# QKV projection of a two-layer trunk: from one product of full matrices to seven products of halves

## What is computed

```python
for i in range(DEPTH):
    hn = rmsnorm(h, attn_norm[i])
    qkv = hn @ w_qkv[i]                                   # 2304 columns
    aq, ak, av, bq, bk, bv, _rest = jnp.split(qkv, QKV_SPLITS + (QKV_WIDTH,), axis=-1)
    ya = sliding_window_sink_attention(aq, ak, av, ...)   # QK-norm, partial rotary (group A)
    yb = chunked_relpos_attention(bq, bk, bv, ...)        # QK-norm, bias by relative position (group B)
    h = h + jnp.concatenate([ya, yb], axis=-1) @ w_o[i]
    h = h + conv_gated_mlp(rmsnorm(h, ffn_norm[i]), w_up[i], conv_w[i], conv_b[i], w_down[i])
    gate = jax.nn.sigmoid(rmsnorm(h, ple_norm[i]) @ w_ple_gate[i])
    h = h + (p[i] @ w_ple_proj[i]) * gate
```

## Time and profile before

| | |
|---|---|
| median of 3 runs | 2497.51 us (2496.66 to 2498.68) |
| the profiled execution | 2496.49 us, its span 2494.7 us |
| PE busy | 2460.4 us, 99% of the span |
| PEld / DVE / ACT / POOL busy | 86% / 54% / 51% / 41% |
| TensorE clock granted | 0.999 of full, 9 in all 40 slices |
| QKV stage, layer 0 | first product at 14.53, last of the four entry transpositions at 220.03 |
| QKV stage, layer 1 | first product about 1253.4, last entry transposition at 1459.60 |

### The profile page before, as it was taken

How to read it: one execution, slowest core, us unless ns; L and a number is a source line. 1 busy time by engine, 2 the same in 40 slices (tenths; PEclk the granted TensorE clock), 3 DMA queues, 4 the chain that set the end, 5 groups by cost and what they waited for, 6 DMA issues and landing times.

```text
span 2494.7 us, 37383 instructions
## 1 busy us (share of the span) xinstructions
PE 2460.4 (99%) x12992; PEld 2150.7 (86%) x12992; DVE 1348.7 (54%) x1876; ACT 1263.3 (51%) x1966; POOL 1034.8 (41%) x783
## 2 busy tenths in 40 slices
PE   8999999999999999999999999999999999999999
PEld 8999998878888888888899999988788888888887
DVE  3114664376656668873341146733856656778732
ACT  4335773465555554344353467734655555533342
POOL 3455241158788850001224442412578878400011
PEclk9999999999999999999999999999999999999999
DMA  4112000313333358431111120003133243573312
GB/s 166 45 51 55 20 15 26 118 51 109 111 95 109 94 172 294 124 109 43 45 39 45 50 53 28 10 26 127 48 112 109 80 125 110 183 268 123 99 46 84
DMA packets 187901, 225.61 MB, mean 90 GB/s; under 512 B 16112, under 2 KB 118896, under 8 KB 187792
## 3 DMA queue, kind: packets, MB, share of 16 engines
q1 hardware_dynamic: 187200, 221.69, 28.1%
q0 software_dynamic: 592, 2.46, 0.3%
HBM read 169.08 MB, written 55.36 MB: 90 GB/s over the span
## 4 chain that ended last, share of the span: by engine, by line
PE 86%; DVE 5%; ACT 4%; issue 3%; POOL 1%; DMA 0%; ACTq 0%; DVEq 0%; POOLq 0%; SPq 0%
PE ps L2179 10%; PE ps L2181 10%; PE ps L2180 10%; PE ps L2637 10%; PE ps L2639 10%; PE ps L2640 10%; PE ps L2663 6%; PE ps L2661 6%; PE ps L2662 6%; PE ps L2413 3%; PE ps L2402 1%; PE ps L2374 1%; PE ps L2506 1%; PE ps L2331 1%; PE ps L2473 1%
## 5 line engine op out<-in xcount | busy, mean ns | idle before, releaser
L885 POOL TENSOR_TENSOR w_hl<-w_raw,w_hl 128x1024 fp32r<-128x1024 f32 x84 | 203.1, 2418 | 989.5 <-ACT w_hl L1076 989.5
L2179 PE MATMUL ps<-w_hl,xT 128*128 128x384 f32 (+1 forms) x1280 | 460.1, 359 | 3.1 <-POOL w_hl L885 1.0
L2181 PE MATMUL ps<-w_hl,xT 128*128 128x384 f32 (+1 forms) x1280 | 456.3, 356 | 0.0
L2180 PE MATMUL ps<-w_hl,xT 128*128 128x384 f32 (+1 forms) x1280 | 456.0, 356 | 0.0
L1076 ACT ACTIVATE w_hl<-w_raw 128x1024 fp32r<-128x1024 f32 x84 | 89.1, 1060 | 430.5 <-PE ps L2181 404.7
L2179 PEld LDWEIGHTS ps<-w_hl,xT 128*128 128x128 f32 x1280 | 240.3, 188 | 24.4 <-issue 2.5
L2181 PEld LDWEIGHTS ps<-w_hl,xT 128*128 128x128 f32 x1280 | 240.2, 188 | 20.2
L2180 PEld LDWEIGHTS ps<-w_hl,xT 128*128 128x128 f32 x1280 | 240.4, 188 | 19.1
L2009 DVE SCALAR_TENSOR_TENSOR ps<-c_up,ccols,ps 128x1023 f32<-128x1023 f32 x84 | 107.8, 1283 | 142.3 <-ACT ps L1430 142.3
L1666 DVE TENSOR_REDUCE q_sum<-sq 128x384 f32 x80 | 44.2, 553 | 251.4 <-ACT sq L1138 251.4
L1988 DVE TENSOR_TENSOR c_up<-ps,kept 128x512 f32<-128x512 f32 x126 | 86.6, 689 | 125.1 <-ACT kept L1389 69.4
(11 more groups left out here) (292 smaller groups left out, 6087.1 us busy)
## 6 DMA issues: line engine op xcount, KB each, us to landing
ad_raw<-v_rows SPq DMA_DIRECT2D x70, 512.0 KB, 3.7
raw_a<-in_w_up SPq DMA_DIRECT2D x44, 512.0 KB, 5.0
raw_g<-in_w_up SPq DMA_DIRECT2D x44, 512.0 KB, 5.3
v_rows<-c_up SPq DMA_DIRECT2D x22, 1024.0 KB, 4.4
w_raw<-in_w_qkv SPq DMA_DIRECT2D x48, 384.0 KB, 3.2
wd_main<-in_w_down SPq DMA_DIRECT2D x30, 512.0 KB, 8.1
v_rows<-hc_g SPq DMA_DIRECT2D x22, 512.0 KB, 5.0
w_raw<-in_w_o SPq DMA_DIRECT2D x16, 512.0 KB, 3.8
```

The lines of the kernel that those rows point to most:

```text
L885: nc.gpsimd.tensor_tensor(w_hl[:, slot % 2, 1, :], w_raw[:, slot % 2, :], w_hl[:, slot % 2, 0, :].bitcast(F), ALU.subtract) \
L2179: nc.tensor.matmul(dst, lhs[:, k, 0, cols], wh, start=first, stop=False)
L2180: nc.tensor.matmul(dst, lhs[:, k, 0, cols], wl, start=False, stop=False)
L2181: return nc.tensor.matmul(dst, lhs[:, k, 1, cols], wh, start=False, stop=last)
```

## The change

The matrix of inputs is cut in quarters A11 (first 512 tokens, first 512 features) to A22, the weights in quarters B11 (first 512 rows, first 1152 columns) to B22, the result in C11 to C22, and C is made from seven products (Strassen's) in the order of `Q_ORDER`. Each product has three steps of 384 columns (21 steps, `m`), each step two slots (42 slots), and each slot 24 matmuls: 4 tiles of tokens, 6 matmuls each. A step fills 4 banks, the next step the other 4.

- Weights: 30 of the 42 slots need the sum or difference of two blocks. SP loads both (384 KB each), POOL sums them in place (`qkv_sum`), then ACT makes the high part and POOL the low part. The first block has three buffers (`w_raw` and the new `w_raw_c`), the second two. The order on POOL is: low of slot s, then sum of slot s+2. Ops of a slot are now 128x768, no longer 128x1024.
- Inputs: h transposed and scaled is kept whole in `x_keep`; for the products 5, 7, 1, 2 and 6 POOL forms the sum of two quarters in two parts (`input_sum`, 128x1024 each), ACT makes the high part (`input_high`) and DVE the low (`input_low`), into a ring of three. Product 4 needs a plain quarter (no sum), product 3 uses A11.
- Results: of each step ACT writes what comes first into a block of C (`first_writes`), DVE adds the rest (`q_add`, 128x384, from PSUM onto the block). Squares are now taken from the finished block in SBUF (`head_squares`).
- The norm's factors of the QK-norm are made in two parts, heads 0 to 23 and the rest.
- `rotate` moves from the projection into group B, two tiles behind the copies of each of the heads 1 to 4. POOL's low of the first slot of `w_o` now stands between the copies of head 0 and those of head 1. The loads of group A's values (`load_values`) move behind the bias of the last head; the load of `ext_in` moves from POOL's queue to SP's.

```diff
-SLOTS = QCHUNKS * 4 + 8 + 10
+Q_ORDER = (3, 5, 7, 4, 1, 2, 6)
+Q_WEIGHTS = {3: ("B12", "B22"), 5: ("B22",), 7: ("B21", "B22"), 4: ("B21", "B11"), 1: ("B11", "B22"),
+             2: ("B11",), 6: ("B11", "B12")}
+Q_INPUTS = {5: ("A11", "A12", 1), 7: ("A12", "A22", -1), 1: ("A11", "A22", 1), 2: ("A21", "A22", 1),
+            6: ("A21", "A11", -1)}
+Q_FIRST = {3: (("C12", 1), ("C22", 1)), 5: (("C11", -1),), 4: (("C21", 1),)}
+Q_ADDS = {5: (("C12", 1),), 7: (("C11", 1),), 4: (("C11", 1),), 1: (("C11", 1), ("C22", 1)),
+          2: (("C21", 1), ("C22", -1)), 6: (("C22", 1),)}
+Q_FINAL = {5: "C12", 1: "C11", 2: "C21", 6: "C22"}
+QSTEPS = 7 * Q_CHUNKS
+O0 = 2 * QSTEPS
...
+            def load_qkv(L, slot):
+                names, n = Q_WEIGHTS[q_product(slot // 2)], q_twos(slot)
+                if len(names) == 2:
+                    if L * Q_TWO + n >= 2:
+                        sp.wait_ge(s_w_sum, L * Q_TWO + n - 1)
+                    sp.dma_start(other_raw(slot).rearrange("p (k n) -> p k n", k=2), qkv_block(L, slot, names[1])) \
+                        .then_inc(other_loaded[slot % 2], 16)
+                sp.wait_ge(s_w_low_ready, L * SLOTS + (slot + 1 if slot < 2 else slot))
+                sp.dma_start(one_raw(slot).rearrange("p (k n) -> p k n", k=2), qkv_block(L, slot, names[0])) \
+                    .then_inc(one_loaded[slot % 3], 16)
...
+                qkv_sum(0)
+                qkv_sum(1)
+                for slot in range(O0):
+                    qkv_low(slot)
                     if slot in between:
                         between[slot]()
+                    if slot % 6 == 2 and slot < O0 - 6 and Q_ORDER[slot // 6 + 1] in Q_INPUTS:
+                        input_sum(2 * (slot // 6 + 1))
+                    if slot and slot % 6 == 0 and Q_ORDER[slot // 6] in Q_INPUTS:
+                        input_sum(2 * (slot // 6) + 1)
+                    if slot + 2 < O0:
+                        qkv_sum(slot + 2)
...
+                def copies(hd):
+                    b = hd % 2
+                    pool.wait_ge(s_fill_ready, L * FILLS + (4 * hd + C_FILL - 4))
+                    if hd == 1:
+                        pool.wait_ge(s_q_rstd_ready, L * 2 + 2)
...
+                for hd in range(B_HEADS):
+                    copies(hd)
+                    if hd == 0:
+                        low(O0)
+                    if 1 <= hd <= TT // 2:
+                        rotate(2 * hd - 2)
+                        rotate(2 * hd - 1)
...
+                for m in range(1, QSTEPS - 1):
+                    qkv_high(L, 2 * m + 1)
+                    first_writes(m - 1)
+                    head_squares(m - 1)
...
+                    qkv_high(L, 2 * m + 2)
+                    if m % 3 and m < QSTEPS - 3:
+                        input_high(2 * (m // 3 + 1) + m % 3 - 1)
...
+                for m in range(1, QSTEPS):
+                    step_adds(m - 1)
+                    i = 2 * (m // 3 + 1)
+                    if m % 3 == 0 and m > 1:
+                        input_low(2 * (m // 3) + 1)
+                    if m < QSTEPS - 1:
+                        step_rest(m - 1)
+                    if m % 3 == 1 and i < 14:
+                        input_low(i)
...
+                for m in range(1, QSTEPS):
+                    for kp in range(2):
+                        slot_ready(2 * m + kp)
+                        if m % Q_CHUNKS == 0:
+                            pe.wait_ge(s_xlow, L * XFILLS + input_number(2 * (m // Q_CHUNKS) + kp))
                         for t in range(4):
+                            if kp == 0:
+                                q_bank_free(m, t)
+                            q_row(m, kp, t)
```

More of the change, by code:

```diff
@@ new lines, in step_rest, with q_mean, q_refined @@
+                def step_rest(m):
+                    for t in range(4):
+                        if len(Q_ADDS.get(q_product(m), ())) > 1:
+                            q_add(m, 1, t)
+                        if q_normed(m):
+                            head_sum(m, t)
+                def q_mean(part, heads):
+                    nc.vector.tensor_scalar(q_sum[:, :, heads], q_sum[:, :, heads], 1.0 / HD, EPS, ALU.mult, ALU.add) \
+                        .then_inc(s_q_mean_ready, 1)
+                def q_refined(part, heads):
+                    dve.wait_ge(s_q_rms_ready, L * 2 + part + 1)
+                    refine(q_rstd[:, :, heads], q_sum[:, :, heads], q_tmp[:, :, heads], 1 + part).then_inc(s_q_rstd_ready, 1)
```

582 lines of the change are left out of this document (392 added, 190 removed).

## The result

Changed kernel: median 2527.36 us (2525.12 to 2530.93, 4 runs); before, on the same chip, 2497.40 (2496.66 to 2498.68, 4 runs). Ratio 1.0121, 95% interval 1.0108 to 1.0134: slower by 30 us, where 7 were forecast, and above the range. The profiled execution took 2526.32 us.

A forecast was written before the change was run, and what follows sets the result against it. PE, busy 99% of the span, was taken as the bound. Layer 0 +2.3 - 1.5 + 4.4 = +5.2, layer 1 +0.8 - 2.2 + 4.4 = +3.0, less 1.0: +7, so 2503.7 profiled, 2504.5 median, range 2490 to 2515.

The forecast's parts named there:

- The waits: Projection, mostly product starts and slot 3: PE waits 12.4 + 5.3 + 4.7 = 22.4 us per layer.
- 204.0: Projection stage length after the change: 174.7 + 5.1 + 1.8 + 22.4 = 204.0 us.
- 48 matmuls take 8.32 us, one 0.1733: Projection: each matmul less saves 0.173 us while helpers keep pace; 25.0 us per layer if PE never waits.
- half a microsecond was to be caught up: Group B: PE has little slack, so half a microsecond of loss per layer is recovered, 1.0 in all.
- Step 1: Slots 3 and 4 wait for the norm's factor: 3.9 us at slot 3 and 0.8 at slot 4.
- Sharing: Product starts: DVE's input low parts and POOL's operations exclude each other on SBUF, 5.3 us more per layer.
- The exit: Projection's end: last entry transposition to first for head 1 takes 8.4 us instead of 4.0, losing 4.4 per layer.
- Rotations at nothing: Group B: rotations, 7.0 us per head, fit in POOL's idle 11.2 before the values' copy, costing nothing.
- late loads: Rival, projection: weight loads land after 4.5 us; at 5.3 the kernel takes 2515 us; chance 0.13.
- POOL did not keep up: Rival, product starts: POOL's operations cost less than scaled, so the waits vanish; 2469 us, chance 0.1.
- the end was not caught up: Rival, projection's end: the wait there is caught up in head 0; -7.8, 2497 us, chance 0.15.
- the sharing was there: Rival, projection: the sharing wait is absent or falls where POOL waits anyway; -10.6, 2494 us, chance 0.17.

The follow-up runs named there:

- experiment 1: Changed kernel with idle TensorE matmuls or transpositions put into its long gaps, no wait removed: 2512.5 us, ratio 1.0060.
- experiment 5: Changed kernel with DVE's low parts of the input sums reading one SBUF operand instead of two: 2519.5 us, ratio 1.0088.

## Why the prediction was wrong

**The waits: right in place and kind, near in size.** Products 7 and 1 wait for DVE, 4.25 and 3.64, the others 1.1 to 1.6, all in the places named. With the clock kept up (experiment 1) the stages are 204.8 and 202.2 against 204.0, but in layer 0 two misses cancel: from slot 2 on a layer has 20.7 us over 4.16 a slot where 22.4 were forecast, and the first two slots of layer 0 have 8.1 (5.4 in layer 1), 2.7 more than in layer 1, which no term of the sum held.

**The step that failed: what a wait costs.** "48 matmuls take 8.32 us, one 0.1733" was read from a kernel in which PE never stood still for long, and the stage was summed as matmuls at that price plus waits. A wait of 3.6 to 5.2 us costs 1.7 to 2.7 more (16.6 over seven of them), as the matmuls in the part of the stretch behind it run at 0.32. Against the 204.0 forecast the stages are 8.3 and 7.3 longer. The first head of each layer is 1.6 longer (17.3 for 15.7) with its 3.4 us at half clock, where half a microsecond was to be caught up and none was. No rival had this mechanism.

The rest of the 22.6 us between 2503.7 and the profiled 2526.3 is small: the exits 0.8 and 0.9, the first product 0.3, the 1.0 that was to be caught up, 0.3 at the end, and 0.6 at the start of layer 1. That last one hides a misreading: before, layer 1's first product starts at 1254.12, not 1253.4, and the stage is 205.5 long, not 206.2:

```profile
1254.12 0.41 PE L2179 MATMUL ps<-w_hl,xT 128*128 128x384 f32 x1 [0.71 <-issue]
```

Counted from head 2 of layer 0, the product now comes 0.7 later, where the forecast in effect had 0.1 (1253.4 + 0.8).

**Step 1: mis-sized.** 3.9 and 0.8 were forecast, 5.2 and about 0 came. Of the 1.6 that the factor came late, 0.8 is the last copy and square (the mean starts 1.7 behind the step's start, for 0.9) and 0.75 the chain from mean to factor, 4.95 for 4.2. The 4.2 was no undisturbed figure either. It has this row, which the earlier trace rows leave out, beside POOL's low part that runs from 36.46 to 38.85:

```profile
36.75 2.13 DVE L1612 TENSOR_TENSOR h_tmp<-h_rms 128x8 f32<-128x8 f32 x1
```

Before, one of the small operations was held up; under POOL's two sums it was two. The sharing was costed for the large operations alone, and the trace of before already showed that it hits small ones.

**Sharing: right in kind and sign.** L1986 takes 1.98 at the median and 1.22 at least; its cost of 5.3 per layer was not measured by itself (experiment 5 did not take it away).

**The exit: nearly right.** 9.2 and 9.3 for 8.4, the copies for head 1 last, as said. The terms given add up to 8.1 (3.7, 1.4, 1.1 and 1.91), not 8.4, and DVE's row of eight operations, begun 1.4 before, would end 4.1 behind the last transposition by its own figures, not 3.7. **Rotations at nothing: right**, the later heads take 15.7 as before. **Rivals:** the loads of the weights landed in 3.4 to 3.8 us at the median, under 4.5, so late loads fall. POOL did not keep up, the end was not caught up, and the sharing was there.

## What to carry to other kernels

Before work is cut from an engine that never waits, price the waits that come in its place twice: their length, and the matmuls behind each at half clock, which lose 0.46 us for each us in which they run so; in this stage waits of up to 1.6 us had none of that behind them. Then look at the order on the helpers before their amount: two swapped calls gave back 17 us, nearly as much as a third less work on POOL (19). And where the profile names a late engine, go back along its own wait, to the engine whose queue is really in the wrong order.
